# A float32 stack of six layers: opening loads in order of use, mixer keys and compression inputs multiplied once, compression weights loaded during the short convolution

## Chip, cores, metric

The kernel runs on one NeuronCore of a Trainium2 chip. The metric is the device time of one execution in microseconds (us).

## What is computed

The input x is 256 tokens of 1024 channels. Four residual blocks come first (a conformer convolution, a forgetting attention, a short convolution, a second conformer), then one block of three attention mixers and a feed-forward layer. Everything is float32. The change touches the start, the short convolution and the input products of the three mixers:

```python
def conformer_conv_mixer(h, w_in, conv_w, conv_b, ln_g, ln_b, w_out):
    val, glu_gate, z = jnp.split(h @ w_in, 3, axis=-1)
    u = val * jax.nn.sigmoid(glu_gate)
    u = causal_depthwise_conv(u, conv_w) + conv_b          # 31 taps
    u = jax.nn.silu(layer_norm(u, ln_g, ln_b))
    return (u * jax.nn.silu(z)) @ w_out

# mixers: h = rms(x), one product h @ w_in, split into
(a_q, a_k, a_v, i_q, i_k, i_w, b_q, b_kv, b_g, c_qkv, mix_g) = _split_last(h @ w_in[layer], IN_SIZES)
# b: two groups of keys and values; kv 0 and 1 are compressed
blk = src[:, cidx] + pos[:, None, :]                       # 15 blocks of 32 tokens, stride 16
kcmp = _rms(einsum("bnlgd,lde->bnge", blk_k, cmp_w[0]), k_gain)
vcmp = einsum("bnlgd,lde->bnge", blk_v, cmp_w[1])
# a: index scores relu(i_q . i_k) * i_w, top 64 tokens of each query
```

## The kernel before

Activations lie transposed, channels on partitions: xT has 8 tiles of 128 x 256. A **unit** is a piece of weight matrix of 1024 rows x 256 columns (1 MB), loaded by SyncE's queue into a ring of three (`ring`). `unit_in` defines one, and SyncE issues a unit's loads when the unit three places earlier has been split or multiplied. A unit has two **halves** of 128 columns. In the first products of the two conformers TensorE (PE) multiplies the raw weights (L671, 8 products of 256 columns for each half). Everywhere else a half is split into a high part (`whi`, made by ScalarE (ACT), L365) and a low part (`wlo`, made by VectorE (DVE) or GpSimd (POOL), L374). Then each of the 8 row tiles takes three products (high x high, high x low, low x high), so 48 products for a unit: L636 to L638 in the first four mixer units, whose input is not yet normalised, L673 to L675 later, L650 to L652 in the gate units between the attention jobs. `whi` and `wlo` hold four halves, so the split runs at most three halves ahead (`ahead`). For units made with `dve=True` the halves alternate between VectorE and GpSimd by the parity of their number in the whole program. Results go to PSUM banks 0 and 1 in turn; `take_bank` waits until the unit two places earlier has been read out.

Each engine runs its own program in the order written; they meet only in semaphores.

**Opening.** SyncE issues 27 loads on one semaphore: x, all constants (`cst`: identity, ones, masks), norm gains, convolution taps and biases as rows, the tables `hot` and `rel_bias`, `b_f_bias`. PE waits for all 27. It transposes x (L2199, 16), then eleven blocks of rows (L2206), then multiplies four bias tables (L2211). VectorE copies x into xT (L2234), the rows into `cols` and `convw` (L2242), and the tables (L2250). Then comes the first conformer: ScalarE squares xT (L538), PE sums over channels (L598), ScalarE takes the root (L563), VectorE the reciprocal (L566) and scales x into sqb (L569), and PE multiplies the units `vg[0..15]`, with a `z` unit after each fourth. For each of the 16 columns VectorE gates (L942) and runs 20 taps (L967 to L972), ScalarE multiplies 11 more (L862), GpSimd adds these (L916), and PE sums the result over channels (L1020, L1026).

**Short convolution.** 16 columns of two units each, all split on ScalarE and VectorE. ScalarE copies one gate (L1527) and takes the SiLU of another (L1537).

**Mixers, input products.** 21 units, in the order of `plan_mixers`: 0 keys of a and index keys, 1 index queries, 2 and 3 queries of a (these four are scaled by the token norm afterwards, on VectorE, L1853), 4 values and gates, 5 and 6 compression inputs (kv 0, kv 1), 7 and 8 queries of b, 9 and 10 keys of b (selected, window), 11 to 16 queries and keys of c, 17 to 20 values. In units 0, 5, 6, 9 and 10 every 64 columns stand twice, so that each head's key lies on both halves of the partitions:

```python
def dup2(c0):
    return [(c0, HD), (c0, HD), (c0 + HD, HD), (c0 + HD, HD)]
```

After unit 4 ScalarE issues three loads of compression weights (L1724, L1725), 512 KB each in runs of 256 bytes, into the part of `wide` where the bias table T comes later. ScalarE copies units 5 and 6 into one buffer `cmp_in` (L1771, L1772), VectorE adds the positions (L1862), and after unit 9 PE multiplies (L2027, L2031). From unit 10 on ScalarE issues the eight loads of T (L1790). The index scores are eight small products, two after each of the units 5 to 8 (L2019); ScalarE takes their ReLU in L1737 (`index_relu`, at the head of the next unit's work, before it reads that unit's result), VectorE weighs and adds them (L1877, L1879) and finds the top 64. Each normalised key or query unit is squared on ScalarE (L1754) and summed on PE (L1980).

## Time and profile before

| | us |
|---|---|
| median of 3 runs | 1635.49 (1634.3 to 1639.01) |
| profiled execution | 1643.84 |
| its span | 1642.0 |
| PE busy | 1592.1 (97%) |
| VectorE, ScalarE, GpSimd busy | 1020.4, 825.8, 506.2 |
| mean granted TensorE clock | 0.988 |

The span runs from the first to the last recorded instruction; the time of an execution is a little longer. Busy PE is not PE at its peak, since matmuls are pipelined. The granted clock is a share of 2.4 GHz: 0.50 is 1.2 GHz. An fp32 product leaves two records (x16 for 8 products), a transpose or a product of split parts one.

### The profile page before, as it was taken

What the parts mean: (1) busy time and instruction counts of PE and PEld (TensorE: products, weight loads), DVE (VectorE), ACT (ScalarE), POOL (GpSimd) and SP (SyncE); (2) the same over time, 40 slices, a digit from 0 to 9 for tenths busy, and PEclk for the clock granted to TensorE, in tenths of its full rate; (3) what the DMA queues carried; (4) which work ended last, traced back from release to release, by engine and by line L of the source; (5) the groups of instructions that cost most, each with busy time, mean ns of one, the idle gap of its engine ahead of it and who ended that gap; (6) DMA issues with size and microseconds to landing.
All of it is one profiled execution on the core that took longest, in us unless ns stands there. A gap on an engine that the chain in (4) does not pass through costs nothing.

```text
span 1642.0 us, 27721 instructions
## 1 busy us (share of the span) xinstructions
PE 1592.1 (97%) x10691; PEld 1448.3 (88%) x10691; DVE 1020.4 (62%) x2120; ACT 825.8 (50%) x1512; POOL 506.2 (31%) x474
## 2 busy tenths in 40 slices
PE   4999999999999999999999999989999999999998
PEld 3888899888888999999888889978887778999998
DVE  3899976544665686665399997643035535775532
ACT  1576665434555454444266665543335645454442
POOL 0577652432222300000067764254311112100033
PEclk8999999999999999999999999998999999999999
DMA  4464354555643566765354536594641212666654
GB/s 132 129 171 129 128 186 152 179 150 132 118 114 129 163 179 182 192 181 185 103 154 129 153 121 201 139 193 125 183 154 52 71 40 84 193 176 186 175 162 125
DMA packets 341478, 240.07 MB, mean 146 GB/s; under 512 B 36673, under 2 KB 328643, under 8 KB 341348
## 3 DMA queue, kind: packets, MB, share of 16 engines
q1 hardware_dynamic: 329880, 231.33, 49.0%
q10 hardware_dynamic: 11468, 6.98, 2.1%
q8 instruction: 85, 1.39, 0.3%
q14 instruction: 45, 0.37, 0.1%
HBM read 236.55 MB, written 1.74 MB: 145 GB/s over the span
## 4 chain that ended last, share of the span: by engine, by line
PE 82%; DVE 9%; ACT 4%; issue 2%; DMA 2%; POOL 1%; SPq 1%; ACTq 0%; DVEq 0%; POOLq 0%
PE bank L671 17%; PE bank L673 7%; PE bank L674 7%; PE bank L675 7%; PE bank L1090 4%; PE bank L1407 3%; PE bank L722 3%; PE bank L724 3%; PE bank L723 3%; PE bank L1408 3%; PE bank L1409 3%; DVE bank L972 2%; PE bank L685 2%; DVE wlo L374 2%; PE bank L1183 2%
## 5 line engine op out<-in xcount | busy, mean ns | idle before, releaser
L374 POOL TENSOR_TENSOR wlo<-ring,whi 128x1024 fp32r<-128x1024 f32 (+3 forms) x116 | 258.7, 2234 | 706.2 <-ACT whi L365 706.2
L365 ACT CAST whi<-ring 128x1024 fp32r<-128x1024 f32 (+3 forms) x357 | 345.6, 986 | 258.2 <-PE bank L675 88.3
L374 DVE TENSOR_TENSOR wlo<-ring,whi 128x1024 fp32r<-128x1024 f32 (+4 forms) x241 | 313.4, 1308 | 242.1 <-ACT whi L365 240.8
L671 PE MATMUL bank<-sqb,ring 128*128 128x256 f32 x1536 | 341.1, 383 | 6.2 <-DVE sqb L569 6.2
L671 PEld LDWEIGHTS bank<-sqb,ring 128*128 128x128 f32 x1536 | 294.9, 192 | 47.8 <-issue 6.9
L916 POOL TENSOR_TENSOR scratch<-scratch 128x256 f32<-128x256 f32 x288 | 200.2, 734 | 379.0 <-ACT scratch L862 368.9
L673 PE MATMUL bank<-xh,whi 128*128 128x256 f32 x960 | 275.3, 287 | 0.3 <-DVE xl L591 0.3
L674 PE MATMUL bank<-xl,whi 128*128 128x256 f32 x960 | 273.5, 285 | 0.0
L675 PE MATMUL bank<-xh,wlo 128*128 128x256 f32 x960 | 273.4, 285 | 0.0
L972 DVE SCALAR_TENSOR_TENSOR bank<-scratch,convw,bank 128x256 f32<-128x256 f32 x576 | 231.1, 481 | 0.0
L673 PEld LDWEIGHTS bank<-xh,whi 128*128 128x128 f32 x960 | 186.2, 194 | 7.2 <-issue 6.0
L674 PEld LDWEIGHTS bank<-xl,whi 128*128 128x128 f32 x960 | 186.4, 194 | 0.0
L675 PEld LDWEIGHTS bank<-xh,wlo 128*128 128x128 f32 x960 | 186.2, 194 | 0.0
L862 ACT ACTIVATE scratch<-scratch,convw 128x256 f32<-128x256 f32 x320 | 144.5, 498 | 22.9 <-POOL scratch L916 22.2
L722 PE MATMUL bank<-y_hi,whi 128*128 128x256 f32 x512 | 147.3, 288 | 2.5 <-POOL wlo L374 2.4
L724 PE MATMUL bank<-y_hi,wlo 128*128 128x256 f32 x512 | 144.9, 283 | 0.0
L723 PE MATMUL bank<-y_lo,whi 128*128 128x256 f32 x512 | 144.8, 283 | 0.0
L1407 PE MATMUL bank<-xh,whi 128*128 128x256 f32 x384 | 110.6, 288 | 0.8 <-DVE qk L1373 0.8
L1408 PE MATMUL bank<-xl,whi 128*128 128x256 f32 x384 | 108.6, 283 | 0.0
L1409 PE MATMUL bank<-xh,wlo 128*128 128x256 f32 x384 | 108.5, 283 | 0.0
L722 PEld LDWEIGHTS bank<-y_hi,whi 128*128 128x128 f32 x512 | 98.2, 192 | 3.5 <-ACT whi L365 2.7
L723 PEld LDWEIGHTS bank<-y_lo,whi 128*128 128x128 f32 x512 | 98.2, 192 | 0.3
(282 smaller groups left out, 2908.5 us busy)
## 6 DMA issues: line engine op xcount, KB each, us to landing
ring<-in_a_w_in_dram SPq DMA_DIRECT2D x64, 512.0 KB, 5.1
ring<-in_b_w_in_dram SPq DMA_DIRECT2D x32, 1024.0 KB, 5.9
ring<-in_c_w_in_dram SPq DMA_DIRECT2D x64, 512.0 KB, 5.4
ring<-in_w_in_dram SPq DMA_DIRECT2D x26, 1024.0 KB, 5.0
ring<-in_w_ffn_in_dram SPq DMA_DIRECT2D x44, 512.0 KB, 5.0
ring<-in_a_w_in_dram SPq DMA_DIRECT2D x16, 1024.0 KB, 5.2
ring<-in_a_w_out_dram SPq DMA_DIRECT2D x16, 1024.0 KB, 5.3
ring<-in_w_ffn_out_dram SPq DMA_DIRECT2D x16, 704.0 KB, 4.5
```

What stands on the lines that cost most here:

```text
L365: nc.scalar.copy(piece(whi, h)[:, :, 0:n], src).then_inc(hi_done, 1)
L374: engine.tensor_tensor(piece(wlo, h)[:, :, 0:n], src, piece(whi, h)[:, :, 0:n].bitcast(F32), ALU.subtract).then_inc(done, 1)
L671: mm = nc.tensor.matmul(o, halves[h][1][:, k, :], sqb[:, k, :], start=(k == 0), stop=(k == KD - 1))
L673: nc.tensor.matmul(o, wh[:, k, :], xh[:, k, :], start=(k == 0), stop=False)
L674: nc.tensor.matmul(o, wh[:, k, :], xl[:, k, :], start=False, stop=False)
L675: mm = nc.tensor.matmul(o, wl[:, k, :], xh[:, k, :], start=False, stop=(k == KD - 1))
L722: nc.tensor.matmul(o, wh[:, k, :], hi[:, kk, :], start=first, stop=False, skip_group_check=True)
L723: nc.tensor.matmul(o, wh[:, k, :], lo[:, kk, :], start=False, stop=False, skip_group_check=True)
L724: mm = nc.tensor.matmul(o, wl[:, k, :], hi[:, kk, :], start=False, stop=end, skip_group_check=True)
L916: nc.gpsimd.tensor_tensor(to, a, tmp[:, (first + i) % 4, :], ALU.add)\
L972: ins = nc.vector.scalar_tensor_tensor(to[:, a, :], src, w, to[:, a, :], ALU.mult, ALU.add)
L1407: nc.tensor.matmul(o, wh, xh[:, k, :], start=first, stop=False, skip_group_check=True)
```

## The change

- **Opening.** The loads get semaphores of their own and come in another order: identity and ones, x in two halves, the gains of the a norms; then the weights of unit 0; seven loads of rows of the first conformer; unit 1; all other rows, tables and the rest of `cst`; unit 2. PE transposes x half by half, then only the gains, and sums the squares (now in bank 7). The rows of the first conformer are transposed ahead of unit 0, all others after unit 0, the tables are multiplied after units 1 and 2. The copies out of PSUM go from VectorE to ScalarE.
- **Compression weights.** ScalarE issues the three loads in the short convolution, at columns 4, 6 and 8, into places that are free there (`qk` and the end of `wide`).
- **Mixers.** 19 units. Unit 0 has 128 columns instead of 256; one `cmp` unit (5) has both compression inputs, and one `keys` unit (8) both keys of b, each column once. The copies out of PSUM write each 64 rows to both halves of the partitions. `cmp_in` has two buffers. What stood at unit 9 to 18 stands one or two places earlier; the index products come after units 4 to 7, the compression products after unit 7, the loads of T at units 8 to 15.

```diff
+        def late_rows_copy(act):
+            act.wait_ge(set_done, 8)
+            nc.scalar.copy(cols[:, 16:88], bank[6][:, 16:88])
+            nc.scalar.copy(cols[:, 184:232], bank[6][:, 184:232]).then_inc(rows_copied, 1)
+            act.wait_ge(set_done, 9)
+            nc.scalar.copy(convw[:, 496:992], bank[3][:, 0:496]).then_inc(rows_copied, 1)
+            act.wait_ge(rows_copied, 4)
+            for i, (src, scale) in enumerate(((FQ, FD ** -0.5), (QK2, HD ** -0.5), (QK2 + 2, HD ** -0.5), (QK2 + 4, HD ** -0.5))):
+                nc.scalar.activation(gq[:, i:i + 1], cols[:, src:src + 1], ACT.Copy, scale=scale).then_inc(gq_done, 1)
...
+        def early_rows(pe):
+            pe.wait_ge(early_rows_loaded, 16 * 7)
+            nc.tensor.transpose(bank[5][:, 0:96], rows[0:96, 1, :], ident[0:96, 0:96]).then_inc(set_done, 1)
+            for i in range(4):
+                mm = nc.tensor.transpose(bank[6][:, 124 * i:124 * i + 124], rows[0:124, 3 + i, :], ident[0:124, 0:124])
+            mm.then_inc(set_done, 1)
...
+                if j == 0 and c == 1:
+                    late_rows_copy(act)
+                    tables_copy(act, (0, 1))
+                if j == 0 and c == 2:
+                    tables_copy(act, (2, 3))
...
             for c in range(KE):
                 proj_T(pe, *n["vg"][c], c == 0, n["ph"])
+                if j == 0 and c == 0:
+                    late_rows(pe)
+                elif j == 0 and c < 3:
+                    tables(pe, (2 * c - 2, 2 * c - 1))
+                elif j == 0 and c == 3:
+                    pe.wait_ge(tab_copied, 4)
...
-            order = [("raw", [(OFF_AK, HD), (OFF_AK, HD), (OFF_IK, HD), (OFF_IK, HD)]),
+            order = [("raw", [(OFF_AK, HD), (OFF_IK, HD)]),
...
-                     ("cmp", dup2(kv[0])), ("cmp", dup2(kv[1]))]
+                      ("cmp", [(kv[0], P), (kv[1], P)])]
...
-            order += [("raw", dup2(kv[2])), ("raw", dup2(kv[4]))]
+            order += [("keys", [(kv[2], P), (kv[4], P)])]
...
+        CMP_AT = {4: 0, 6: 1, 8: 2}
+        def cmp_weights(act, i):
+            w0 = t["nsa_cmp_w_2"][0]
+            dst = cwv if i == 2 else cwk[:, :, i * HD:(i + 1) * HD]
+            act.dma_start(dst, w0[i // 2].rearrange("(l q) d e -> (q d) l e", q=2)).then_inc(cmpw_loaded, 16)
...
+                elif kind == "keys":
+                    src = b[:, :].rearrange("p (a t) -> p a t", t=S)
+                    for g2 in range(B_G):
+                        for half in range(2):
+                            ins = nc.scalar.copy(qk[64 * half:64 * half + 64, KS:KW + 1, g2, :], src[64 * g2:64 * g2 + 64, :, :])
+                    ins.then_inc(m_raw, 1)
+                    act.wait_ge(m_raw, i - 3)
+                    for s in SLOTS[i]:
+                        square_heads(qk[:, s, :, :].rearrange("p a t -> p (a t)"))
...
-                    q = count["cmp"]
-                    wait(act, k_blk, q)
-                    bb = b[:, :].rearrange("p (g t) -> p g t", g=B_G)
-                    nc.scalar.copy(cmp_in[0:64, :, :], bb[0:64, :, :]).then_inc(k_in, 1)
-                    nc.scalar.copy(cmp_in[64:P, :, 0:S - 1], bb[64:P, :, 1:S]).then_inc(m_raw, 1)
+                    for q in range(2):
+                        for g2 in range(B_G):
+                            rows_ = slice(64 * g2, 64 * g2 + 64)
+                            nc.scalar.copy(cmp_in[q][0:64, g2, :], src[rows_, q, :])
+                            ins = nc.scalar.copy(cmp_in[q][64:P, g2, 0:S - 1], src[rows_, q, 1:S])
+                        ins.then_inc(k_in if q == 0 else m_raw, 1)
```

PE's instructions at the start of the program, before (x16 are sixteen transposes of x; `qk` holds the rows and tables there, `cst` the identity):

```order
L2199 MATMUL bank<-cst,wide 128x128 x16
L2206 MATMUL bank<-cst,qk 128x88
L2206 MATMUL bank<-cst,qk 128x96
L2206 MATMUL bank<-cst,qk 128x48
L2206 MATMUL bank<-cst,qk 128x124 x8
L2211 MATMUL bank<-qk,small 16x384
L2211 MATMUL bank<-qk,small 4x384 x3
L598 MATMUL bank<-sqb,cst 128x256 x8
L671 MATMUL bank<-sqb,ring 128x256 x64
```

PE at the same place in the changed program:

```order
L2312 MATMUL bank<-cst,wide 128x128 x16
L2315 MATMUL bank<-cst,qk 128x16
L660 MATMUL bank<-sqb,cst 128x256 x8
L589 MATMUL bank<-cst,qk 128x96
L591 MATMUL bank<-cst,qk 128x124 x4
L733 MATMUL bank<-sqb,ring 128x256 x16
L597 MATMUL bank<-cst,qk 128x88
L598 MATMUL bank<-cst,qk 128x48
L600 MATMUL bank<-cst,qk 128x124 x4
L733 MATMUL bank<-sqb,ring 128x256 x16
L612 MATMUL bank<-qk,small 16x384
L612 MATMUL bank<-qk,small 4x384
```

The sums of squares follow the transposes of x directly, and five blocks of rows stand before unit 0; the other six and the tables stand between the units.

ScalarE's instructions in the mixers from unit 4's values on, before (`small` takes the sigmoid of the gates, L1737 is the index ReLU):

```order
L1765 COPY vb<-bank 128x2x220
L1776 ACT_TABLE_LOAD
L1776 ACTIVATE small<-vb 128x48
L1724 DMA wide<-in_nsa_cmp_w_dram 128x16x64 x2
L1725 DMA wide<-in_nsa_cmp_w_dram 128x16x64
L365 CAST whi<-ring 128x1024
L1771 COPY vb<-bank 64x512
L1772 COPY vb<-bank 64x2x255
L365 CAST whi<-ring 128x1024 x2
L1737 ACTIVATE wide<-bank 128x128 x2
L1771 COPY vb<-bank 64x512
```

ScalarE at the same place in the changed program:

```order
L1855 COPY vb<-bank 128x2x220
L1867 ACT_TABLE_LOAD
L1867 ACTIVATE small<-vb 128x48
L368 CAST whi<-ring 128x1024
L1813 ACTIVATE wide<-bank 128x128 x2
L1862 COPY vb<-bank 64x256
L1863 COPY vb<-bank 64x255
L1862 COPY vb<-bank 64x256
L1863 COPY vb<-bank 64x255
L1862 COPY scratch<-bank 64x256
```

The three loads are gone from this place, the first ReLU comes ahead of the compression copies, and eight smaller copies (the second four into `scratch`) do what four did in two units.

## Rows read from the trace of the kernel before

**Rows 1.** The page: busy us, then the chain that ended last.

```profile
PE 1592.1 (97%) x10691; PEld 1448.3 (88%) x10691; DVE 1020.4 (62%) x2120; ACT 825.8 (50%) x1512; POOL 506.2 (31%) x474
...
PE 82%; DVE 9%; ACT 4%; issue 2%; DMA 2%; POOL 1%; SPq 1%; ACTq 0%; DVEq 0%; POOLq 0%
```

**Rows 2.** Timeline of the opening: start us, us, engine, line, what, idle before.

```profile
16.94 3.68 PE L2199 MATMUL bank<-cst,wide 128*128 128x128 f32 x16 [16.94 <-DMA small<-in_b_f_bias_dram]
...
18.10 0.69 DVE L2234 COPY xT<-bank 128x512 f32<-128x512 f32 x1 [18.10 <-PE bank L2199]
...
21.57 1.28 ACT L538 ACT_TABLE_LOAD   x1 [21.57 <-DVE cols L2242]
...
22.87 2.19 ACT L538 ACTIVATE sqb<-xT 128x512 f32<-128x512 f32 x4
```

**Rows 3.** The chain of waits, 0 to 60 us: start us, us, what.

```profile
20.62 2.35 PE bank L2206 x11
22.97 3.37 PE bank L2211 x8
...
27.02 5.99 PE bank L598 x16
...
36.04 24.06 PE bank L671 x97
```

**Rows 4.** Activity by stretch; after the busy times: PEclk, DMA share, GB/s.

```profile
17.00:20.00 3.00, 3.00 (x15) 3.00 (x16) 1.58 (x3) 0.00 (x0) 0.00 (x0) 1.00 1.20 291
...
29.00:31.00 2.00, 2.00 (x7) 1.55 (x5) 0.00 (x0) 0.00 (x0) 0.00 (x0) 0.50 0.00 0
...
39.00:41.00 2.00, 2.00 (x6) 1.55 (x6) 0.00 (x0) 0.00 (x0) 0.00 (x0) 0.50 0.00 0
```

**Rows 5.** PE's waits from 36 to 240 us; VectorE's second and third gate.

```profile
PE bank L1020 <- DVE wide L950: 0.3, 1, 0.3
...
53.44 0.42 DVE L942 TENSOR_TENSOR scratch<-bank,scratch 128x256 f32<-128x256 f32 x1 [1.27 <-ACT scratch L838]
...
61.60 0.42 DVE L942 TENSOR_TENSOR scratch<-bank,scratch 128x256 f32<-128x256 f32 x1
```

**Rows 6.** PE in the mixers' input products: its waits, then two timeline rows.

```profile
PE bank L2019 <- ACT wide L1737: 6.2, 2, 3.3
...
1091.39 0.28 PE L675 MATMUL bank<-xh,wlo 128*128 128x256 f32 x1
...
1106.06 0.58 PE L673 MATMUL bank<-xh,whi 128*128 128x256 f32 x1
```

**Rows 7.** ScalarE there: the first two weight issues, the third, the delayed ReLU.

```profile
L1724 ACTq DMA_DIRECT2D wide<-in_nsa_cmp_w_dram x2: 442/2444/4447, 1079.0 to 1079.5; - x2
...
1083.95 6.01 ACTq L1725 DMA_DIRECT2D wide<-in_nsa_cmp_w_dram x1
...
1104.12 0.28 ACT L1737 ACTIVATE wide<-bank 128x128 f32<-128x128 f32 x1 [4.24 <-DVE wide L1877]
```

**Rows 8.** VectorE there: scalings of x, positions added (twice two), first index score.

```profile
1053.48 8.96 DVE L614 SCALAR_TENSOR_TENSOR sqb<-xT,cols,rr 128x256 f32<-128x256 f32 x8
...
1092.22 4.36 DVE L1862 TENSOR_TENSOR vb<-vb,cols 128x240 f32<-128x240 f32 x2 [10.94 <-ACT vb L1772]
1097.89 3.99 DVE L1862 TENSOR_TENSOR vb<-vb,cols 128x240 f32<-128x240 f32 x2 [1.31 <-ACT vb L1772]
1101.71 2.31 DVE L1877 TENSOR_SCALAR wide<-wide,vb 128x128 f32<-128x128 f32 x1
```

**Rows 9.** DMA in the first 8 us: GB/s in 40 slices of 0.2 us.

```profile
GB/s 0 0 0 0 0 0 0 0 0 143 102 205 61 307 451 389 389 451 410 430 389 492 389 369 332 423 427 366 412 283 113 73 76 15 49 41 36 46 3 87
```

**Rows 10.** Short convolution: SyncE's waits from 600 to 750 us, activity of 20 us.

```profile
SPq L242 <- DVE wlo L374: 126.9, 28, 6.0
...
640.00:660.00 20.00, 20.00 (x169) 20.00 (x168) 13.67 (x20) 8.82 (x13) 0.00 (x0) 1.00 0.65 180
```

**Rows 11.** PE's waits from 1222 to 1420 us (attention and branches), low parts.

```profile
PE bank L650 <- DVE wlo L374: 2.0, 2, 1.8
```

More of the change, by code:

```diff
@@ L530, in program @@
         GAIN = [0, 2, 3, 1, 4, 5]
-        rms_bank = [bank[7 if ph == 2 else 3 if ph == 1 else 2] for ph in range(NPH)]
+        rms_bank = [bank[7 if ph in (0, 2) else 3 if ph == 1 else 2] for ph in range(NPH)]
         def rms_square(act, ph, g):
@@ new lines, in program, with tables_copy @@
+        TABLES = ((0, 16), (16, 4), (20, 4), (24, 4))
+        def tables_copy(act, vs):
+            for v in vs:
+                act.wait_ge(tab_done, v + 1)
+                nc.scalar.copy(tabs[0:TABLES[v][1], v, :], bank[(2, 7)[v % 2]][0:TABLES[v][1], 0:TABLE]).then_inc(tab_copied, 1)
+        def early_rows(pe):
[4 more added lines that the diff above has]
+            mm.then_inc(set_done, 1)
@@ new lines, in late_rows @@
+        def late_rows(pe):
+            pe.wait_ge(late_rows_loaded, 16 * 14)
+            pe.wait_ge(rows_copied, 3)
+            nc.tensor.transpose(bank[6][:, 0:88], rows[0:88, 0, :], ident[0:88, 0:88])
+            nc.tensor.transpose(bank[6][:, 184:232], rows[0:48, 2, :], ident[0:48, 0:48]).then_inc(set_done, 1)
+            for i in range(4):
+                mm = nc.tensor.transpose(bank[3][:, 124 * i:124 * i + 124], rows[0:124, 7 + i, :], ident[0:124, 0:124])
+            mm.then_inc(set_done, 1)
@@ new lines, in tables @@
+        def tables(pe, vs):
+            if vs[0] == 0:
+                pe.wait_ge(table_loaded, 32)
+                pe.wait_ge(set_pool, 2)
+            else:
+                pe.wait_ge(rest_loaded, 32)
+                pe.wait_ge(tab_copied, 2)
+            for v in vs:
+                h0, nh = TABLES[v]
+                nc.tensor.matmul(bank[(2, 7)[v % 2]][0:nh, 0:TABLE], small[0:33, 224 + h0:224 + h0 + nh],
+                                 hot[:, v * TABLE:(v + 1) * TABLE], start=True, stop=True).then_inc(tab_done, 1)
@@ L1732, in index_relu @@
             def index_relu(i):
-                for m in range(2 * (i - 6), 2 * (i - 5)):
+                for m in range(2 * (i - 5), 2 * (i - 4)):
                     act.wait_ge(i_s, m + 1)
@@ L1852, in mixers_dve @@
                 group_done(dve, u)
[L1853 removed]
+                if i == 0:
+                    for a in range(2):
+                        from_ = slice(64 * a, 64 * a + 64)
+                        for half in range(2):
+                            ins = nc.vector.tensor_tensor(qk[64 * half:64 * half + 64, 0, a, :], bank[g % 2][from_, 0:S],
+                                                          rr[from_, 0:S], ALU.mult)
+                    ins.then_inc(m_ev, 1)
+                    continue
+                nc.vector.tensor_tensor(qk[:, SLOTS[i][0], :, :], bank[g % 2][:, :].rearrange("p (a t) -> p a t", t=S),
                                         rr_both(), ALU.mult).then_inc(m_ev, 1)
@@ L2160, in _, with load @@
-            for i in range(8):
-                load(rows[0:124, 3 + i, :], flat[124 * i:124 * i + 124, :])
-            load(hot, t["hot"])
-            load(small[0:32, 224:224 + HEADS2], t["rel_bias_2"])
-            load(fb, t["b_f_bias"].rearrange("a h -> h a"))
-            assert n[0] == SETUP_LOADS
+            def load(dst, src, done):
+                sp.dma_start(dst, src).then_inc(done, 16)
+            xv = t["x"][0].rearrange("(b p) d -> p b d", p=P)
+            flat = t["a_conv_w"].rearrange("j a (k p) -> (j a k) p", p=P)
@@ L2200, in _ @@
                 mm.then_inc(set_done, 1)
-            for i in range(11):
-                if i >= 4:
-                    pe.wait_ge(set_used, i - 3)
-                nr = ROWS_OF[i]
-                nc.tensor.transpose(bank[4 + i % 4][:, 0:nr], rows[0:nr, i, :], ident[0:nr, 0:nr]).then_inc(set_done, 1)
-            for v, (h0, nh) in enumerate(((0, 16), (16, 4), (20, 4), (24, 4))):
-                if v == 0:
-                    pe.wait_ge(x_done, 4)
-                nc.tensor.matmul(bank[v][0:nh, 0:TABLE], small[0:33, 224 + h0:224 + h0 + nh], hot[:, v * TABLE:(v + 1) * TABLE],
-                                 start=True, stop=True).then_inc(tab_done, 1)
-            pe.wait_ge(set_dve, 5)
-            pe.wait_ge(tab_copied, 4)
+            pe.wait_ge(gain_loaded, 16)
+            nc.tensor.transpose(bank[4][:, 0:16], rows[0:16, 0, :], ident[0:16, 0:16]).then_inc(set_done, 1)
             conf_pe(pe, conf0)
```

207 lines of the change are left out of this document (109 added, 98 removed).

## Prediction

> **What bounds the kernel now.** I read the busy table and the chain of waits first [rows 1]. TensorE (PE) works in 97% of the 1642.0 us span and carries 82% of the chain, so an edit is worth what it takes out of PE's instruction stream or out of PE's waits; work taken from another engine counts only where PE waits for it. The change touches three stretches, read in this order: the opening up to the first projection, the short convolution, and the input products of the mixers.
>
> In the opening the landing of the last of SyncE's 27 loads (b_f_bias) lets PE start at 16.94 [rows 2]. PE transposes x (3.68 us), then [rows 3] eleven blocks of rows (2.35), makes four bias tables (3.37), sums squares (5.99), and after square root, reciprocal and first scaled tile starts the first projection at 36.04. The activity table [rows 4] shows full clock while PE transposes x, half (0.50, 1.2 GHz) during the sums and again at 39 to 41.
>
> In the first conformer block PE then waits 0.3 us in all up to 240 us [rows 5]: PE sets the pace. But VectorE's taps end just in time, that 0.3 being PE's wait for VectorE. So I have to check that VectorE does not become the bound.
>
> In the mixers PE stands still twice, 6.2 us together (3.3 and so 2.9), both times for a ReLU on ScalarE [rows 6]. The first wait goes back to ScalarE's own queue: the three issues of compression weights hold ScalarE, 0.44, 4.45 and 6.01 us, from 1079.0 to 1090 [rows 7]. The second goes back to VectorE, which adds positions in four instructions (8.35 us together) and then multiplies the first index score (2.31), while ScalarE waits 4.24 for it [rows 7, 8].
>
> **The opening.** Now PE waits only for the identity, half of x, the other half. Before, 1.4 MB (x and all constants) had moved by about 6 us, first bytes at 1.8, 390 to 490 GB/s once going [rows 9]. Adding up those slices, the 0.64 MB of identity, ones and first half are there at about 4.0 and 1.15 MB at about 5.3; with a few tenths for completion I take 4.4 and 5.7. Sixteen transposes of 0.23: 4.4 to 8.1, VectorE's copies (0.69) following, the last at 8.6. ScalarE loads its table after the first copy (1.28) and squares 4 x 0.55 [rows 2]: 7.4 to 9.6. PE's sums start at 8.1 and take 5.99 at half clock [rows 3], about 3.4 at full. The end of the sums to the first projection was 3.02 (33.02 to 36.04) and stays. So the projection starts at 14.6 with full clock in the sums and at 17.1 with half; at half clock in the rows are only stretches after the dense transposes of x, with small tables and pauses between; now the sums follow the transposes at once, so I go nearer the first: 15.0, **21.0 us earlier**. The rows needed before it (seven loads, issued behind unit 0 by about 8 us, 0.45 each) land by about 11; their five transposes fit into the 3 us in which PE waits for the scale anyway. Unit 0's weights, 1 MB behind x, are in by 9.
>
> The other six transposes (6 of the 11, 1.4) and the four tables (3.37 for 8 records, the last of them at half clock; I take 2.6, bound 3.4) now stand between units 0 to 3, in PE's stream: **+4.0**. Does VectorE allow it? It waited 1.27 for its second gate and nothing for the third [rows 5]. Its second gate comes 1.4 later. ScalarE has its row and table copies (about 2.7) behind the second sigmoid, which makes the third gate another 0.4 late; the fourth is free. VectorE loses 1.8 where PE loses 4.0, so PE stays the bound, and VectorE's 5 us of row and table copies, taken away, were hidden already except in what is counted. Weights of units 1 and 2 are issued behind 7 and 18 small loads, at about 9 and 17 us, and wanted at 22 and 30. Opening: −21.0 + 4.0 = **−17.0** (bounds −20 and −11: no half clock at all; everything 3 us later and the sums at half).
>
> By the Trainium skill (TensorE: Matmul & The Clock Gate, Part 1) an idle PE is held at 1.2 GHz and only work raises it. The rows at 17 to 20 say otherwise for this start: after 17 us of nothing the granted clock is 1.00 and 15 transposes take 3.00 us [rows 4]. By the page the 16 transposes would cost 3.7 more and the opening would give 13.3; I go by the row.
>
> **The short convolution.** The three weight issues come after ScalarE's gate of columns 4, 6 and 8, some 23 us apart. The first issue of a burst costs 0.44, the later ones 4.4 and 6.0 because they stand behind it [rows 7]; alone I take 0.44 each. ScalarE is busy 8.8 of 20 us there and waits for PE [rows 10], so nothing: 0, bound +10 (three times what 4.4 would push past its slack). Their 1.5 MB go through DMA engines that are 65% busy; SyncE waits for a free ring slot for nearly the whole time [rows 10], a late landing of 3 us being covered by nearly two units of split weights. 0.
>
> **The mixers.** A unit of 48 products costs 48 x 20/169 = 5.7 us at full clock [rows 10]. One unit of keys, one of compression inputs and one half unit go: 120 products, **−14.2**. Sums of squares (13) and compression products are as many as before. What gives back:
> - The first unit is 2.8 shorter, but VectorE frees the second unit's bank, which PE's fourth needs, only after eight scalings (8.96 us, to 1062.4) [rows 8], longer than the unit of 5.7 that PE has in the meantime; ScalarE stands behind the same event with the split weights. I credit 1.5 of the 2.8: **+1.3**, bounds 0 and 2.8.
> - The wait for the index ReLU stays. Let the compression unit end at T. ScalarE now has eight copies of 64 rows, near 0.3 each: first input at T+1.3, second at T+2.4. VectorE's four additions follow each other to T+9.7. From the start of its first score multiplication (1101.71) to the next unit on PE (1106.06) it took 4.35 [rows 6, 8]: T+14.0. Before, from the end of the second compression unit (1091.67) to 1106.06 it was 14.4. So the two waits turn into one of about 5.5 to 6 us and the sum is 0.4 better: **−0.4**, bounds −3 (VectorE's additions at their shortest, 1.3 each) and +2.
> - Keys: four copies of 64 rows x 512, two squares and the row spreading meet in one unit, 5.7 us on ScalarE beside 6.9 of PE, and the split ahead is 3 halves. 0, bound +1.5. No time is won from the removed ScalarE stall beyond what the wait above holds.
> - Five halves fewer turn the parity by which VectorE and GpSimd share the low parts in the attention, branches and the last output product. PE waits 2.0 us for VectorE's low parts there [rows 11]; I take 0, bounds that much either way.
>
> Mixers: −14.2 + 1.3 − 0.4 = **−13.3** (−17 to −7).
>
> **Sum.** −17.0 − 13.3 = −30.3 against a span of 1642.0: 1611.7. The profiled execution took 1643.84, 8.35 over the median of the three shown, 1635.49; against that median **1605.2 us**.
>
> **Rivals.**
> 1. *The opening runs at half clock*, from the first transpose, as the idle before it would have it: +3.7 for transposes, +2.5 for sums: 1611. Against: the full clock at 17 to 20. For: it fell to half twice soon after. That is the page's rule cited above. 0.12.
> 2. *ScalarE's weight issues only move.* If each costs 4.4 to 6 in the short convolution too and PE is short of split weights: up to +10, 1615. Against: the ring and ScalarE both wait for PE there. This is also the case in which the third part does not do what it says. 0.05.
> 3. *The index wait grows or the keys unit starves PE*: if VectorE's additions meet GpSimd's splits all along (2.6 each, as the longest did) and the spreading delays the high parts: +4 to +7, 1610 to 1612. 0.13.
> 4. *Slower*: PE's clock. The stream of the opening is now cut up by tables of 33 rows between units, and half clock costs 6.9 us per unit of the conformer. The gain of 30.3 is gone if 4.4 units more run at 1.2 GHz than now; if the first eight do, +55: 1660. Against: between the tables stand 16 long products each, and three units in a row ran without a wait behind the start before [rows 5]. 0.02.
>
> The forecast has 0.68, with a range of its own of 1598 to 1612. The predicted time is its middle. For 8 in 10 the range takes in rivals 1 and 3 and the low bound of the opening: 1594 to 1614. A measurement of this kernel can tell about 0.3% (5 us) from no change. Faster by more than that: all but rival 4 and a rest of unknown kind, 0.95; within: 0.02; slower: 0.03.
>
> **What would show it.** Right: first transpose near 4.4 us, first projection near 15, PE without a wait between, the first product of the conformer's output some 17 us earlier than now (219.4), issues of compression weights below 0.6 us each in the short convolution and no PE wait beside them, one wait of 5 to 6 us for the index ReLU, and the mixers' first scores another 13 earlier. Wrong: an issue in the short convolution above 4 us with PE waiting for a high part, VectorE ahead of nobody (PE waiting over 2 us at the end of the first conformer's taps), more than one long index wait, or a granted clock of half beyond 25 us.

## The result and the profile after

| | before | after |
|---|---|---|
| median, us | 1634.89 (1631.41 to 1639.01, 4 runs) | **1617.78** (1611.64 to 1620.07, 4 runs) |
| profiled execution, its span | 1643.84, 1642.0 | 1615.93, 1614.1 |
| mean granted TensorE clock | 0.988 | 0.989 |

The ratio is 0.9882 with a 95% interval of 0.986 to 0.9904: 19.3 us faster, by the interval 15.7 to 22.9 (the medians of the table differ by 17.1). Faster by more than 0.3% was right. The 1605.2 us was not: 1617.8 lies 5.8 us above the forecast's own range (1598 to 1612) and 3.8 above the wider one (1594 to 1614).

The page of the changed kernel, as [rows 1]: busy us, then the chain that ended last.

```profile
PE 1575.9 (98%) x10572; PEld 1431.5 (89%) x10572; DVE 1013.3 (63%) x2102; ACT 825.8 (51%) x1527; POOL 504.5 (31%) x470
...
PE 83%; DVE 9%; ACT 5%; issue 2%; DMA 1%; POOL 1%; DVEq 0%; SPq 0%; ACTq 0%; POOLq 0%
```

PE is still the bound. Since it is, the start times of its stages say where the time went (differences of the two profiles, us, minus is gained):

| stretch on PE | forecast | measured |
|---|---|---|
| up to the conformer's first output (219.43, now 202.46) | −17.0 | −17.0 |
| from there to the mixers' input products (1045.87, now 1029.62) | 0 | +0.7 |
| mixers' input products to the first attention scores (1224.72, now 1187.47) | −13.3 | −21.0 |
| attention to the first branch unit (1376.98, now 1348.82) | 0 | **+9.1** |
| from there to the last transposes (1635.51, now 1607.61) | 0 | +0.3 |

Two rows are wrong, and the sum (−27.9) is not the timed difference (−19.3). The experiments are about both. The first row hits its forecast exactly, and that is partly luck: the profile of the kernel before that it starts from was a long one (see the part alone, below).

**The opening.** The timeline of PE in the changed kernel, as [rows 2, 3]:

```profile
5.84 3.57 PE L2312 MATMUL bank<-cst,wide 128*128 128x128 f32 x16 [5.84 <-DMA wide<-in_x_dram]
9.34 0.24 PE L2315 MATMUL bank<-cst,qk 16*128 16x16 f32 x1
9.71 3.72 PE L660 MATMUL bank<-sqb,cst 128*128 128x256 f32 x16
13.77 0.30 PE L589 MATMUL bank<-cst,qk 96*128 96x96 f32 x1 [0.34 <-DMA qk<-in_a_conv_w_dram]
...
16.47 7.74 PE L733 MATMUL bank<-sqb,ring 128*128 128x256 f32 x28 [1.97 <-DVE sqb L631]
```

The two halves of x came 1.4 us later than I had put the first one; the transposes and the sums then ran at full clock (3.72 for 16 records, 5.99 before). The activity table shows where the clock fell:

```profile
10.00:13.00 3.00, 3.00 (x15) 2.64 (x15) 0.25 (x4) 2.56 (x5) 0.00 (x0) 1.00 0.73 206
17.00:19.00 2.00, 2.00 (x6) 1.61 (x5) 2.00 (x6) 0.00 (x0) 0.00 (x0) 0.50 0.18 52
19.00:21.00 2.00, 2.00 (x9) 1.73 (x9) 0.09 (x1) 0.00 (x0) 0.00 (x0) 0.89 0.75 192
```

Full at the start, after 5.8 us of nothing; half (0.50) from about 16.0, that is from within the 1.97 us in which PE waits for the first scaled tile, to about 19.4. Waits with half clock behind them return below.

**The short convolution.** ScalarE's three issues of compression weights, duration in ns min/median/max:

```profile
L1600 ACTq DMA_DIRECT2D qk<-in_nsa_cmp_w_dram x2: 380/408/437, 616.0 to 639.1; - x2
L1600 ACTq DMA_DIRECT2D wide<-in_nsa_cmp_w_dram x1: 374/374/374, 662.1 to 662.1; - x1
```

0.4 us each where the burst cost 0.44, 4.45 and 6.01 [rows 7]. Their cost here is 0, as forecast.

**The mixers' input products.** PE's waits there (in total, times, longest), then VectorE's position additions and first index score, then GpSimd in the same stretch, as [rows 6, 8]:

```profile
PE bank L2120 <- ACT wide L1813: 2.5, 2, 1.7
```

```profile
1068.20 1.29 DVE L1962 TENSOR_TENSOR vb<-vb,cols 128x240 f32<-128x240 f32 x2 [6.19 <-ACT vb L1863]
1069.73 1.31 DVE L1962 TENSOR_TENSOR vb<-scratch,cols 128x240 f32<-128x240 f32 x2 [0.23 <-ACT scratch L1863]
1070.87 2.47 DVE L1977 TENSOR_SCALAR wide<-wide,vb 128x128 f32<-128x128 f32 x1
```

```profile
1065.79 2.39 POOL L377 TENSOR_TENSOR wlo<-ring,whi 128x1024 fp32r<-128x1024 f32 x1 [4.33 <-ACT whi L368]
1070.85 4.70 POOL L377 TENSOR_TENSOR wlo<-ring,whi 128x1024 fp32r<-128x1024 f32 x2 [2.67 <-ACT whi L368]
```

The four additions took 2.60 us, not 8.35, and the waits fell from 6.2 to 2.5 (in a second profile of the kernel before, below, they were 3.0). The additions fell where GpSimd does nothing (1068.18 to 1070.85); in the kernel before they stood beside its splits:

```profile
1091.18 7.53 POOL L374 TENSOR_TENSOR wlo<-ring,whi 128x1024 fp32r<-128x1024 f32 x3 [10.44 <-ACT whi L365]
1099.01 4.93 POOL L374 TENSOR_TENSOR wlo<-ring,whi 128x1024 fp32r<-128x1024 f32 x2 [0.30 <-ACT whi L365]
```

**The attention.** PE's waits from the first scores to the first branch unit, before (first fence) and after:

```profile
PE bank L1157 <- ACT scratch L1166: 3.7, 12, 0.6
```

```profile
PE bank L1167 <- DVE small L1178: 4.0, 5, 1.8
PE bank L1234 <- ACT scratch L1243: 3.8, 11, 0.6
PE bank L1234 <- DVE scratch L1220: 0.4, 1, 0.4
```

New is a wait of the score products (L1167) for VectorE's pass over earlier scores (L1178), which reads them out of PSUM, adds a bias and takes the maximum. The longest one in PE's timeline, and VectorE ahead of it:

```profile
1203.83 1.64 PE L1167 MATMUL bank<-qk 64*128 64x128 f32 x4 [1.82 <-DVE small L1178]
```

```profile
1202.00 1.23 DVE L377 TENSOR_TENSOR wlo<-ring,whi 128x1024 fp32r<-128x1024 f32 x1 [3.33 <-ACT whi L368]
1203.14 0.28 DVE L1178 CUSTOM_DVE_ANT_0 scratch<-bank,wide 128x128 f32<-128x128 f32 x1
```

VectorE stands idle for 3.33 us, because the next thing in its program is the split of a weight half (L377), and ScalarE has not rounded that half yet; the scores that PE needs read out of PSUM stand behind it. The other four waits are 0.54 us each, where VectorE's split (1.22) stands ahead of the scores without waiting itself. Of the change nothing touches this place but the parity: five split halves fewer ahead of it, so the halves of each mixer unit that went to GpSimd go to VectorE and the other way round. I call that the swap.

### The profile page after: what moved, and what is told of

It reads as the page before. It is cut to its first block, busy times and chain, and to the rows that moved or that the text cites. A ratio compares the mean times of both kernels' runs of the same rounds, so it can differ in the third digit from the quotient of the medians.

```text
span 1614.1 us, 27456 instructions
## 1 busy us (share of the span) xinstructions
PE 1575.9 (98%) x10572; PEld 1431.5 (89%) x10572; DVE 1013.3 (63%) x2102; ACT 825.8 (51%) x1527; POOL 504.5 (31%) x470
## 4 chain that ended last, share of the span: by engine, by line
PE 83%; DVE 9%; ACT 5%; issue 2%; DMA 1%; POOL 1%; DVEq 0%; SPq 0%; ACTq 0%; POOLq 0%
PE bank L733 17%; PE bank L735 7%; PE bank L736 7%; PE bank L737 7%; PE bank L1167 4%; PE bank L1484 3%; PE bank L784 3%; PE bank L786 3%; PE bank L785 3%; PE bank L1485 3%; PE bank L1486 3%; DVE bank L1040 2%; PE bank L747 2%; DVE wlo L377 2%; ACT whi L368 1%
## 5 line engine op out<-in xcount | busy, mean ns | idle before, releaser
L377 POOL TENSOR_TENSOR wlo<-ring,whi 128x1024 fp32r<-128x1024 f32 (+3 forms) x112 | 256.8, 2297 | 695.0 <-ACT whi L368 695.0
L368 ACT CAST whi<-ring 128x1024 fp32r<-128x1024 f32 (+3 forms) x352 | 340.2, 985 | 244.0 <-PE bank L737 83.0
L377 DVE TENSOR_TENSOR wlo<-ring,whi 128x1024 fp32r<-128x1024 f32 (+4 forms) x240 | 310.5, 1302 | 234.8 <-ACT whi L368 233.2
L735 PE MATMUL bank<-xh,whi 128*128 128x256 f32 x928 | 265.4, 286 | 0.3 <-DVE xl L653 0.3
L736 PE MATMUL bank<-xl,whi 128*128 128x256 f32 x928 | 263.8, 284 | 0.0
L737 PE MATMUL bank<-xh,wlo 128*128 128x256 f32 x928 | 263.7, 284 | 0.0
L735 PEld LDWEIGHTS bank<-xh,whi 128*128 128x128 f32 x928 | 179.3, 193 | 5.8 <-issue 5.3
L736 PEld LDWEIGHTS bank<-xl,whi 128*128 128x128 f32 x928 | 179.5, 193 | 0.0
L737 PEld LDWEIGHTS bank<-xh,wlo 128*128 128x128 f32 x928 | 179.4, 193 | 0.0
L1484 PE MATMUL bank<-xh,whi 128*128 128x256 f32 x384 | 110.6, 288 | 0.8 <-DVE qk L1450 0.8
L1485 PE MATMUL bank<-xl,whi 128*128 128x256 f32 x384 | 108.6, 283 | 0.0
L1486 PE MATMUL bank<-xh,wlo 128*128 128x256 f32 x384 | 108.6, 283 | 0.0
L1199 ACT ACTIVATE scratch<-scratch,small 128x128 f32<-128x128 f32 (+1 forms) x120 | 50.9, 425 | 94.4 <-DVE small L1189 94.3
```

Of the source, the lines that this page charges most:

```text
L368: nc.scalar.copy(piece(whi, h)[:, :, 0:n], src).then_inc(hi_done, 1)
L377: engine.tensor_tensor(piece(wlo, h)[:, :, 0:n], src, piece(whi, h)[:, :, 0:n].bitcast(F32), ALU.subtract).then_inc(done, 1)
L735: nc.tensor.matmul(o, wh[:, k, :], xh[:, k, :], start=(k == 0), stop=False)
L736: nc.tensor.matmul(o, wh[:, k, :], xl[:, k, :], start=False, stop=False)
L737: mm = nc.tensor.matmul(o, wl[:, k, :], xh[:, k, :], start=False, stop=(k == KD - 1))
L1484: nc.tensor.matmul(o, wh, xh[:, k, :], start=first, stop=False, skip_group_check=True)
```

## Experiments

**The swap, undone and alone.** `e1_parity` is the changed kernel with the old assignment from the mixer units on; `e2_flip` is the kernel before with only the swap.

```diff
-                halves.append((u, ap, k, n, dve == ALL or (dve and len(halves) % 2 == 0)))
+                halves.append((u, ap, k, n, dve == ALL or (dve and (len(halves) + flip[0]) % 2 == 0)))
...
+            flip[0] = 1
             n["mix"] = [(group((m_mix, 4 * i + d + 1)), unit_in(w, [(OFF_MIX + br * D + d * 2 * P, 2 * P)], True))
```

> The changed kernel, with one thing put back: from the twelve mixer units on, the halves that VectorE splits and those that GpSimd splits are again the ones of the kernel before (the changed kernel has five split halves fewer ahead of them, an odd number, so the two engines have swapped). Theory A (the swap is what the mixer attention and the branches lost, 9.1 us between 1187.47 and 1348.82 in the changed profile against 1224.72 and 1376.98 before): the stretch from the mixer attention's start to the first branch unit is 152.3 us again instead of 161.4, the wait L1167 for DVE's L1178 (4 times 1.8 us) is gone, and the time is 8 to 9 us under the changed kernel's 1617.8, near 1609, 26 to 28 under the kernel before. Theory B (the loss comes from what the mixers section leaves behind, such as TensorE arriving 37 us earlier than VectorE and ScalarE can follow, or a lower granted clock): the stretch stays at 159 to 162 us and the time at 1616 to 1619.

> The kernel before with nothing but the swap: from the mixer units on, VectorE splits the halves that GpSimd split, and the other way round. Theory A (the swap costs the 9.1 us): the stretch from the mixer attention to the first branch unit grows from 152.3 us to about 161, the wait L1167 for VectorE's copy of the softmax appears, and the time is 8 to 9 us over the kernel before, ratio about 1.005. Theory B: 0, within 2 us of the kernel before, and the stretch at 152 to 153 us. If only part of the loss appears here, the swap needs the new mixers section ahead of it to cost in full.

Measured: `e1_parity` 1606.20 us (1605.45 to 1607.75, 4 runs) against 1636.90 of the kernel before on that chip, ratio 0.9821 (0.9803 to 0.984). `e2_flip` 1644.61, ratio 1.0053 (1.0033 to 1.0074): 8.7 us slower by nothing but who splits which half. The stretch from the first scores to the first branch unit takes 151.5 us (1189.44 to 1340.90) with the swap undone and 162.3 (1223.31 to 1385.60) with the swap alone, against 152.3 before and 161.4 after. PE's waits there, `e1_parity` first, then `e2_flip`:

```profile
PE bank L1236 <- ACT scratch L1245: 4.3, 12, 1.0
```

```profile
PE bank L1092 <- DVE small L1103: 4.0, 5, 1.8
PE bank L1159 <- ACT scratch L1168: 3.7, 11, 0.6
PE bank L1159 <- DVE scratch L1145: 0.4, 1, 0.4
```

The wait comes and goes with the swap, and theory A holds in both directions. But 4.0 us of waits are not all of it. The activity tables of the changed kernel give most of the rest (PEclk is the third number from the right); `e1_parity` has 1.00 in both of the windows that answer to these:

```profile
1200.00:1212.50 12.50, 10.35 (x49) 8.67 (x50) 5.17 (x24) 6.77 (x20) 2.45 (x1) 0.73 0.26 85
...
1237.50:1250.00 12.50, 11.53 (x71) 9.50 (x70) 5.58 (x27) 7.92 (x26) 3.43 (x1) 0.86 0.26 86
```

```profile
1201.90:1214.40 12.50, 11.27 (x71) 8.86 (x72) 6.81 (x31) 7.10 (x20) 2.39 (x1) 1.00 0.27 85
...
1239.40:1251.90 12.50, 12.29 (x86) 10.22 (x86) 8.02 (x45) 5.80 (x27) 1.21 (x1) 1.00 0.27 85
```

The missing clock is worth 0.27 x 12.5 + 0.14 x 12.5 = 5.1 us. The stretch is 9.9 us longer than in `e1_parity` (161.4 against 151.5): 3.9 are waits (8.2 against 4.3 in all), 5.1 are clock, and 0.9 I can't place. Against the first profile of the kernel before the difference is only 9.1, because that one had 1.7 us of missing clock of its own in its attention. The wait of 1.8 us is followed by half clock from 1203.9 to 1210.7, which costs twice as much as the wait. The second stretch, 1244.8 to 1248.2, stands behind a wait of only 0.54.

**The two other parts alone.** `e3_open` is the kernel before with the new opening, `e4_mix` with the new mixers and the moved weights (and so with the swap), `e8_cmpw` with the moved weights only.

```diff
# e3_open, core
-            load(xnat, t["x"][0].rearrange("(b p) d -> p b d", p=P))
...
+            def load(dst, src, done):
+                sp.dma_start(dst, src).then_inc(done, 16)
# e4_mix, core
-            order = [("raw", [(OFF_AK, HD), (OFF_AK, HD), (OFF_IK, HD), (OFF_IK, HD)]),
+            order = [("raw", [(OFF_AK, HD), (OFF_IK, HD)]),
# e8_cmpw (and in e4_mix)
+                if c in CMP_AT:
+                    cmp_weights(act, CMP_AT[c])
...
-                if i == 4:
-                    cmp_weights()
```

> The kernel before with the new opening alone (loads in order of use, early transposes, the first projection from 16.5 us on); the mixers and the swap as before. By the landmarks of the two profiles the conformer's first output comes 17.0 us earlier. Theory A (nothing behind it takes that back): 17 us under the kernel before, ratio 0.9896, and the mixers inputs take 178.9 us from 1045.87 less 17. Theory B (the profiled run of the kernel before was a slow draw of 8 us and the 17 hold some of that): a timed gain of 9 to 14 us while its profile shows the same 17.0 at the conformer's output.

> The kernel before with the other two parts alone: the mixer keys and compression inputs multiplied once, and the compression weights loaded in the short convolution. The opening is as before; the swap of VectorE's and GpSimd's halves comes with it, since the five halves are fewer here too. Theory A (sum of the profile's stretches): mixers inputs 21.0 us shorter, attention and branches 9.1 longer, so 11 to 12 us under the kernel before, ratio 0.993. Theory B (the shorter index waits and the 21.0 belong to the earlier opening or to chance): mixers inputs 13 us shorter as I had forecast, and 4 us under the kernel before in all.

> The kernel before with one part alone: the compression weights are loaded during the short convolution, and ScalarE's three issues in the mixers (0.44, 2.44 and 4.45 us) are gone from there; the keys and compression inputs are multiplied as before, no swap. Theory A (ScalarE's stall is part of what TensorE waits for at the index scores, 6.2 us in two waits): 3 to 4 us less in the mixers inputs (175 instead of 178.9) and in the time. Theory B (the position additions on VectorE, 8.35 us, hold the index scores whatever ScalarE does): mixers inputs 178 to 179 us and no difference that shows.

Measured: `e3_open` 1620.59, ratio 0.9906 (0.9889 to 0.9923): −15.4 us, by the interval −12.6 to −18.2; its conformer output came 17.4 us earlier than in the first profile of the kernel before. The interval holds the 17 of theory A and part of B's 9 to 14. The second profile of the kernel before (`e9_again`, below) tells them apart: its conformer output came at 216.52, not 219.43, and `e3_open`'s at 202.06, so the opening gives 14.5, and theory B's reason holds, if not its number. The first profile has 0.50 in the window 39 to 41 [rows 4], behind the first projection's start; that half clock, some 3 us worth, the second one doesn't have. `e4_mix` 1630.89, ratio 0.9968 (0.9956 to 0.998): −5.2 us. That was a miss of theory A's 11 to 12, which had trusted the long first profile, and B's 4 is only near because the swap is in it: the mixers' input products take 159.4 us, the attention 161.2. `e8_cmpw` 1632.23, ratio 0.9975 (0.9964 to 0.9986): −4.1 us, theory A (its mixers' input products take 169.5 us, against 178.9 in the first profile of the kernel before and 174.1 in the second, below; the 2.44 us in its expectation is the median of the first two issues, not an issue: they took 0.44, 4.45 and 6.01). PE's waits in its mixers' input products are down from 6.2 [rows 6] to

```profile
PE bank L2018 <- ACT wide L1738: 0.7, 1, 0.7
```

and the position additions show the same as above: 4.01 us for two beside GpSimd, 1.29 for two without it.

The parts add up. Take the swap (+8.7) out of −5.2: the mixers' edits alone are worth −13.9 (give or take 4, by the two intervals), of which the moved weights are −4.1 and everything else −9.8. The −9.8 is not the price of the products left out. From `e8_cmpw` to `e4_mix` the mixers' input products go from 169.5 us at a granted clock of 0.99 to 159.4 at 0.97; at full clock that is 167.8 and 154.6, so 13.2 less, although the index waits grow from 0.7 to 2.4. The products gave about what 120 of them cost in PE's stream (14.2), and more half clock took some of it back. With the opening, −15.4 − 13.9 = −29.3 us; `e1_parity`, which is these two without the swap, measured 0.9821 x 1636.9, also −29.3. With the swap −20.6, against −19.3 for the change.

**What about the swap costs: the place, or GpSimd beside VectorE?** The swap changes two things. VectorE's half now stands where ScalarE has only just got to it and ahead of the scores; and GpSimd's half falls beside VectorE's softmax work and takes 3.4 us instead of 2.35. `e5_late_swap` keeps the swap and moves VectorE's splits behind the scores and the division of the job before; `e6_late_parity` does that with the swap undone.

```diff
                 if j < NJ:
-                    for f, a in filler_at(j):
-                        lo_dve_to(dve, hs(n["mix"][f][1])[a] + 1)
                     scores_dve(dve, AM, j)
...
                     norm_dve(dve, AM, j - 1)
+                if j < NJ:
+                    for f, a in filler_at(j):
+                        lo_dve_to(dve, hs(n["mix"][f][1])[a] + 1)
```

> The changed kernel, swap and all, with VectorE's order in the mixer attention altered: a job's scores and the division of the job before stand ahead of its split of a mixer half, where the split stood first. Theory A (what costs is the place: the swap put the half that VectorE splits right behind ScalarE's rounding and ahead of the scores that TensorE waits for): the waits of L1167 for VectorE (4.0 us in all) and the half clock behind them (the windows of the changed trace show 0.73 and 0.86 where the unswapped ones show 1.00) go, the attention takes 151 to 153 us, and the time is 1606 to 1610. Theory B (what costs is that GpSimd's halves now fall beside VectorE's softmax work and both are slower, 3.4 us for GpSimd's in place of 2.35): the attention stays at 159 to 162 us, the time at 1616 to 1619.

> The changed kernel with the swap undone and VectorE's splits behind the scores and the division, both edits together. Theory A (the place ahead of the scores is all that costs, and with the swap undone nothing waits there any more): equal to the kernel with the swap undone, 1606.2, within 2 us. Theory B (a split ahead of the scores costs in every second job even there): 2 to 4 us less, 1602 to 1604.

`e7_pool_only` leaves all mixer halves to GpSimd; `e10_pool_brief` keeps VectorE's queue as changed and lets GpSimd do an eighth of its mixer halves (the rest of these low parts is left out).

```diff
# e7_pool_only
-... unit_in(w, [(OFF_MIX + br * D + d * 2 * P, 2 * P)], True))
+... unit_in(w, [(OFF_MIX + br * D + d * 2 * P, 2 * P)], False))
# e10_pool_brief, in lo_to
+                    if not mine and u in brief:
+                        n = 16
+                        src = src[:, :, 0:n]
```

> The changed kernel with all halves of the twelve mixer units split by GpSimd, none by VectorE (the branch units and the feed-forward as in the changed kernel). Two halves then fall to GpSimd in each pair of jobs, 2 times 2.4 to 3.4 us in some 17 us. Theory A (place in VectorE's queue): VectorE never waits for ScalarE's rounding there and TensorE's wait for the scores goes, attention 151 to 154 us, time 1607 to 1611. Theory B (the two engines in each other's way): GpSimd runs twice as long beside VectorE, and the attention takes 162 us or more, the time 1618 or more.

> The changed kernel, swap and all, but GpSimd subtracts only 128 of the 1024 columns of its twelve mixer halves (the rest of the low parts is left out), so that it is hardly ever busy in the mixer attention; VectorE's queue is as in the changed kernel, with its split ahead of the scores. Theory A (the place in VectorE's queue costs the 9 us): TensorE's waits of L1167 for VectorE stay at 3 to 4 us, the attention takes 159 to 161 us, the time is 1614 to 1618. Theory B (VectorE's softmax work held up beside GpSimd's halves costs them): the waits and the half clock go, the attention takes 151 to 153 us and the time is 1606 to 1609. In between, both do.

| | us | ratio to before | first scores to branches, us |
|---|---|---|---|
| `e5_late_swap` | 1606.70 | 0.9825 (0.9808 to 0.9842) | 152.8 |
| `e6_late_parity` | 1611.37 | 0.9852 (0.9833 to 0.987) | 156.3 |
| `e7_pool_only` | 1619.57 | 0.9899 (0.9882 to 0.9916) | 160.0 |
| `e10_pool_brief` | 1615.74 | 0.9884 (0.9868 to 0.9901) | 160.3 |

`e10_pool_brief` settles it. With GpSimd busy for 11.7 us of the stretch instead of 27.8, the new wait is the same and the time is too, within the spread of the runs:

```profile
PE bank L1172 <- DVE small L1183: 4.0, 5, 1.8
PE bank L1239 <- ACT scratch L1248: 3.7, 12, 0.6
```

So the place in VectorE's queue costs the 9 us, and moving the splits from there with the swap left in gives them back (`e5_late_swap`, windows all at 1.00). GpSimd's 3.4 us were real and cost nothing. So were 4.2 us that VectorE lost in one line of small operations (L1189, 7.6 us in all, 3.4 in `e10_pool_brief`). That is not so in general: in `e7_pool_only`, where neither theory's numbers came (160.0 us, between the two), the wait for the scores is gone as theory A has it, but GpSimd has two halves in a row, 4.7 us, small operations of VectorE beside them take up to 2.25 us, and VectorE's divisions (L1220) are what PE ends up waiting for:

```profile
PE bank L1234 <- ACT scratch L1243: 5.9, 11, 0.9
PE bank L1234 <- DVE scratch L1220: 3.2, 4, 1.6
```

`e6_late_parity` was a miss: I expected no difference to 1606.2 and it lost 5. With the old assignment the half that PE multiplies first in the attention is VectorE's, and moved behind the scores it comes too late, once:

```profile
PE bank L714 <- DVE wlo L378: 2.4, 1, 2.4
```

```profile
1191.20:1203.80 12.60, 9.98 (x48) 8.46 (x48) 4.50 (x22) 4.61 (x14) 0.00 (x0) 0.73 0.26 83
```

Again a wait of about 2 us, and again 0.73, worth 0.27 x 12.6 = 3.4. But here the clock fell at 1194.7, while PE stood still until 1196.28, and half clock costs nothing in a wait: of the 3.4 some 0.8 lie there. That makes 2.4 + 2.6 = 5.0 us for one late half, where the whole stretch is 4.8 longer than in `e1_parity` (156.3 against 151.5).

**Second profiles of both kernels.**

> The kernel before once more, for a second profile of it. Theory A (the first profile, span 1642.0, was a long draw: the granted clock was at half in more stretches than in most runs; over the runs so far the product of span and mean clock stays near 1620 while the span goes from 1631 to 1642): this profile's product is 1618 to 1622 again, and its span is longer or shorter than 1635 by what its clock lost. Theory B (the first profile did something else that takes time): the product differs by more than 5 us between the two profiles.

> The changed kernel once more, for a second profile of it. Theory A (the waits in the mixer attention are a matter of order, so the same in each run): L1167 waits for VectorE 4.0 us in 5 waits again, the attention takes 159 to 162 us, and the product of span and mean clock is 1596 to 1598, 23 us under the 1620 of the kernel before. Theory B (they were a chance of the first profile): the attention takes under 156 us here.

`e11_after_again` (span 1614.0) shows the same five waits, 4.0 us together, the attention at 161.3 us, and 0.73 and 0.86 in the same two windows. `e9_again`, the kernel before, had a span of 1631.1 with a mean clock of 0.992, against 1642.0 with 0.988. Span times mean clock, the time as it would be at full clock, is 1618.1 and 1622.3; what is left is the time lost to the clock, 13.0 and 19.7. So 6.7 of the 10.9 us between the two profiles are clock and 4.2 are other time, above all the index wait (6.2 in the first, 3.0 in the second); theory A holds for the larger part. Over the timed runs, the means of each run's span split in this way (the clock has three digits, 0.8 us; half clock while PE waits is counted as lost, though it costs nothing):

| kernel, runs | median us | full-clock time, mean | lost to the clock, mean |
|---|---|---|---|
| before, 17 | 1636.9 | 1619.9 | 15.1 |
| after, 4 | 1617.8 | 1596.8 | 18.2 |
| swap alone, 6 | 1644.6 | 1625.6 | 17.8 |
| opening alone, 5 | 1620.6 | 1605.8 | 12.6 |
| after, swap undone, 4 | 1606.2 | 1592.2 | 12.4 |
| after, splits behind the scores, 4 | 1606.7 | 1595.1 | 9.6 |

The full-clock time of a kernel varies by 0.3 to 1.6 us from run to run (standard deviation), while the spans of the kernel before go from 1631 to 1642: most of the spread is how much of the time is at half clock. By this table the change took 23.1 us out and gave 3.1 back in clock, 20.0 in all, which agrees with the timed 19.3; the 27.9 between the first two profiles had a long draw on one side.

## Why the prediction was right and wrong

- **The bound**, PE, and "an edit is worth what it takes out of PE's stream or waits": right.
- **The opening, −17.0**: within its bounds; the part alone gives −15.4 (12.6 to 18.2), and the 17.0 of the two first profiles is luck in part. The projection starts at 16.47 and not at 15.0. By those two profiles only 2.6 us were given back up to the conformer's output, but from projection to output the kernel before took 183.4 us in the first profile and 180.5 in the second, and `e1_parity`, whose opening projection has no half clock, took 184.5: 4.0 given back, as forecast. Rival 1 (half clock from the first transpose) did not happen: full clock until PE waited. The rule of the Trainium skill ("TensorE: Matmul & The Clock Gate", Part 1), weighed in the prediction, is not what the rows show at this start, and the trace before had shown it.
- **The short convolution, 0**: right, and rival 2 is out. Rival 3 did not come either: the position additions met no split of GpSimd's at all.
- **The mixers, −13.3**: without the swap −13.9, so the sum was right, but not all its terms. "No time is won from the removed ScalarE stall beyond what the wait above holds" failed: the moved weights alone give 4.1. "The two waits turn into one of 5.5 to 6" failed: they became 0.8 and 1.7, because the additions were sized at the 8.35 us that they take beside GpSimd. I had 1.3 us each as a bound on the low side and took the other end without asking what made the 2.1 of [rows 8]. The 14.2 for the products holds in PE's stream; that the sum came out is luck, since the gain from the waits and what the clock took back, which the forecast didn't have, nearly cancel.
- **The parity, 0 with bounds of 2**: this is the step that broke the forecast. It measured +8.7 us (5.4 to 12.1). I took its price from PE's waits for low parts [rows 11], which is what it costs if a half comes late. (These were not all: in the same stretch PE waits 3.3 us more in the output product behind the branches, L707. Together with GpSimd's 0.4 that makes 5.7 before and 5.8 after, so there the swap did cost nothing.) What mattered was what stands *behind* the half in VectorE's program: the scores of a job, and ahead of it an event on ScalarE that, for the other half of the unit, comes later. The prediction counted the halves and looked at no place where one stands. The trace of the kernel before has the order in which VectorE works there.
- **The clock**: rival 4 looked for it in the opening. In the opening 1.7 us of it came after all (0.50 at 17 to 19); the larger loss came in the attention, 5.1 us behind a single kind of wait.

With the swap undone, 1606.2 us, the forecast of 1605.2 would have held as a number, with the terms of the waits still wrong.

## What to carry to other kernels

Where work is dealt out by counting (every second piece to the other engine), removing an odd number of pieces upstream re-deals everything downstream: pin the assignment, or look at each engine's program behind the edit, above all at what stands behind a piece that waits for a third engine. Pieces that others need later belong behind results that PE needs now, but each piece has its own deadline: `e5_late_swap` gained by that move, `e6_late_parity` lost by it. Both `e1_parity` and `e5_late_swap` are faster than the change as made, 29.3 and 28.6 us under the kernel before. A wait of about 2 us on a busy PE cost up to three times its length here, with the half clock behind it, and in other places no more than its length. Read the clock column, and a second profile of the same kernel, before believing a difference of two single profiles.

## What the runs showed of the hardware

- **Some VectorE and GpSimd instructions hold each other up for a whole instruction.** The first index score took 2.47 us when it started at 1070.87, beside a GpSimd split started at 1070.85; in `e3_open`, with GpSimd idle when it started at 1085.52, it took

```profile
1085.52 0.26 DVE L1956 TENSOR_SCALAR wide<-wide,vb 128x128 f32<-128x128 f32 x1
```

  and the position additions take 0.65 us each alone and about 2.1 beside it. In the other direction, `e10_pool_brief` has GpSimd's small split at 0.55 us when only the last 0.2 us of a VectorE split lie beside it, and at 1.52 when it starts together with VectorE's split of 1.22 (1223.61):

```profile
1202.28 0.55 POOL L381 TENSOR_TENSOR wlo<-ring,whi 128x128 fp32r<-128x128 f32 x1 [16.64 <-ACT whi L369]
1223.62 1.52 POOL L381 TENSOR_TENSOR wlo<-ring,whi 128x128 fp32r<-128x128 f32 x1 [20.80 <-ACT whi L369]
```

  VectorE's passes over scores out of PSUM are not held: 0.28 and 0.42 us each beside a running split. The Trainium skill ("SBUF — State Buffer", "SBUF: two separate sides") has the rule: a pair of ports is shared, and a GpSimd instruction, or a VectorE one that is in a 2-port mode or (against a GpSimd one that reads SBUF) has two SBUF inputs, locks it for its whole length. These traces agree with it (the additions and splits have two SBUF inputs, the passes over scores one; that the index score is in a 2-port mode no run shows), and the prediction should have used it.
- **Half clock (1.2 GHz) often comes with a short wait of PE, but the wait's length does not decide it.** The 1.8 us wait in the attention had half clock behind it in all five profiles that have the wait (worth 3.4 us in four, 1.7 in `e4_mix`), the 1.97 us in the opening and the 2.4 in `e6_late_parity` had it too, and so had one wait of 0.54 in the same five. Against that, `e7_pool_only` waits 1.57 us in its attention and has 1.00 throughout, and a wait of 1.6 us between 984 and 1003 us, which all thirteen profiles have, never brought it. It also comes without a wait: in all thirteen profiles beside or just behind the 64 products of 30 columns of the compression (in the kernel before from 1127.3 to 1134.2, the products standing at 1122.35 to 1128.6). What decides was not tried.
- **A load's issue takes longer behind large loads on its queue**: SyncE's issue of one small row took 3.16 us directly behind the 1 MB of unit 0, where the next two rows took 0.42 each; the first row behind the 1 MB of unit 1 took 2.35. ScalarE's weight issues had shown the same in their burst [rows 7]. What it waits for inside the queue no run shows.

```profile
3.77 3.16 SPq L2242 DMA_DIRECT2D qk<-in_a_conv_b_dram  x1
```
